# Two-layer decoder trunk with routed experts: the shared expert's first-tile up projection moved into the third quad of experts

## The reference, cut to what matters

```
def moe_ffn(x, router_w, router_b, w_gate, w_up, w_down, s_gate, s_up, s_down):
    scores = sigmoid(x @ router_w)                    # 64 experts, 8 groups
    ...                                               # 4 groups, then 8 experts for each token
    for each expert e and its tokens:
        hb = silu(xb @ w_gate[e]) * (xb @ w_up[e])    # 1024 -> 256
        y[tok] += (hb @ w_down[e]) * gate             # 256 -> 1024
    shared = (silu(x @ s_gate) * (x @ s_up)) @ s_down
    return y + shared
```

## Time and profile before

| what | value |
|---|---|
| median of three runs | 1256.37 us |
| profiled execution | 1257.92 us |
| its span in the profile | 1256.2 us |
| TensorE busy | 1201.1 us (96%) |
| VectorE, ScalarE busy | 397.9 us, 293.9 us |
| mean granted TensorE clock | 0.989 |
| read from HBM | 445.75 MB, 356 GB/s over the span |

### The profile page before, as it was taken

One profiled execution on the slowest core, in us unless ns is written; L12 is line 12 of the kernel. 1 busy time (PEld: TensorE's weight loads), 2 busy tenths in 40 slices (PEclk: granted clock), 3 DMA queues, 4 the chain that ended last, 5 costly groups with the idle time before them and its releaser, 6 DMA issues.

```text
span 1256.2 us, 17136 instructions
## 1 busy us (share of the span) xinstructions
PE 1201.1 (96%) x6956; PEld 560.9 (45%) x6956; DVE 397.9 (32%) x892; ACT 293.9 (23%) x648; POOL 28.5 (2%) x104
## 2 busy tenths in 40 slices
PE   8998999999999999999979999999999999999995
PEld 5776753434343434434336565343434333343431
DVE  3666374212221212222143656421212211221214
ACT  3354331112121212211122343111212111121212
POOL 1005000000000000000000000000000000000000
PEclk9999999999999999999989999999999999999998
DMA  9408068999999999999993657799999999999993
GB/s 369 167 12 330 6 246 368 416 426 425 430 427 426 428 427 427 428 428 428 428 380 106 268 201 293 292 409 429 430 426 428 429 424 429 427 426 430 428 426 131
DMA packets 45024, 447.72 MB, mean 356 GB/s; under 512 B 8096, under 2 KB 9504, under 8 KB 18848
## 3 DMA queue, kind: packets, MB, share of 16 engines
q1 hardware_dynamic: 44368, 446.29, 84.9%
q10 hardware_dynamic: 592, 0.53, 0.2%
HBM read 445.75 MB, written 1.05 MB: 356 GB/s over the span
## 4 chain that ended last, share of the span: by engine, by line
PE 83%; DMA 8%; DVE 5%; ACT 2%; issue 1%; DVEq 0%; SPq 0%
PE psum L411 32%; PE psum L516 16%; DMA w_up_ring<-in_moe_up 8%; PE psum L497 5%; PE psum L427 4%; PE psum L2376 4%; PE psum L2225 4%; PE psum L1246 3%; PE psum L614 2%; PE psum L476 2%; PE psum L648 1%; PE psum L1729 1%; PE psum L2382 1%; PE psum L1557 1%; DVE moe_h L1083 1%
## 5 line engine op out<-in xcount | busy, mean ns | idle before, releaser
L411 PE MATMUL psum<-w_up_ring,moe_x_selected 128*64 128x512 f32 x2048 | 452.8, 593 | 7.6 <-DMA w_up_ring<-in_moe_up 7.5
L411 PEld LDWEIGHTS psum<-w_up_ring,moe_x_selected 128*64 128x64 f32 x2048 | 149.3, 137 | 298.9 <-issue 286.3
L516 PE MATMUL psum<-w_down_ring,moe_hT 128*64 128x512 f32 x960 | 219.2, 598 | 0.0
L1083 DVE SCALAR_TENSOR_TENSOR moe_h<-moe_silu,moe_slot_gate,psum 128x256 f32<-128x256 f32 x64 | 30.7, 480 | 392.7 <-ACT moe_silu L834 392.5
L834 ACT ACTIVATE moe_silu<-psum 128x256 f32<-128x256 f32 x64 | 24.6, 384 | 429.7 <-PE psum L411 429.7
L516 PEld LDWEIGHTS psum<-w_down_ring,moe_hT 128*64 128x64 f32 x960 | 65.2, 136 | 123.4 <-issue 107.4
L1088 DVE TENSOR_TENSOR moe_out_low<-psum,moe_out_high 128x512 fp32r<-128x512 f32 x64 | 44.2, 691 | 213.1 <-ACT moe_out_high L846 213.1
L846 ACT CAST moe_out_high<-psum 128x512 fp32r<-128x512 f32 x64 | 37.5, 585 | 129.3 <-PE psum L516 129.3
L1090 DVE TENSOR_TENSOR moe_out_low<-psum,moe_out_high 128x512 fp32r<-128x512 f32 x64 | 44.2, 690 | 63.6 <-ACT moe_out_high L848 63.6
L427 PE MATMUL psum<-moe_match,moe_x_high 128*128 128x256 f32 x224 | 60.9, 307 | 2.8 <-ACT moe_x_selected L823 2.8
L497 PE MATMUL psum<-moe_out_high,moe_matchT 32*128 32x512 f32 x496 | 62.4, 494 | 0.0
(11 more groups left out here) (536 smaller groups left out, 1062.5 us busy)
## 6 DMA issues: line engine op xcount, KB each, us to landing
w_up_ring<-in_moe_up SPq DMA_DIRECT2D x128, 2048.0 KB, 16.5
w_down_ring<-in_moe_down SPq DMA_DIRECT2D x60, 2048.0 KB, 16.6
w_up_ring<-in_ev_columns SPq DMA_DIRECT2D x4, 2048.0 KB, 17.3
w_up_ring<-in_od_w_in SPq DMA_DIRECT2D x4, 2048.0 KB, 17.6
w_up_ring<-in_ev_out SPq DMA_DIRECT2D x2, 2048.0 KB, 8.1
moe_first_down<-in_moe_down SPq DMA_DIRECT2D x2, 2048.0 KB, 10.0
w_up_ring<-in_od_w_out SPq DMA_DIRECT2D x2, 2048.0 KB, 7.7
ln_gain_bias<-in_ln_g SPq DMA_DIRECT2D x4, 512.0 KB, 7.0
```

The costliest lines, as they stand in the source:

```text
L411: last = nc.tensor.matmul(k.psum[e * SLOTS:(e + 1) * SLOTS, 6, :], xsel[:, kk, own:own + SLOTS], up_view(par, e, kk), start=kk == 0, stop= ...
L516: last = nc.tensor.matmul(k.psum[e * SLOTS:(e + 1) * SLOTS, bank, :], hT[:, j * P + e * SLOTS:j * P + (e + 1) * SLOTS], places[e][:, j, ha ...
L1083: nc.vector.scalar_tensor_tensor(h[:], silu[:], slot_gate[:, i:i + 1], up_ps[:, FE:2 * FE], ALU.mult, ALU.mult).then_inc(s.h, 1)
```

## The change

Tile 0's up projection of the shared expert leaves the routing and `first_pair()`. It is done in one piece of eight matmuls in quad 2 (`SHARED_FIRST`), ahead of `pe_up` of pair i=1, in the way in which tile 1's is done in quad 3, and in the same bank 5. ACT's silu and DVE's product move there too. In layer 0 the transfer of the weights is issued after the fourth pair's second down weights. Quad 2 is written out; the loop ahead of it has one turn left. In `first_pair()` the transposition of the matching (L482) now stands ahead of the wait for `h`. In layer 1 no transfer moves; the matmuls move as in layer 0.

```diff
-SHARED_UP, SHARED_DOWN = 3, 4
+SHARED_FIRST, SHARED_UP, SHARED_DOWN = 2, 3, 4
...
-    shared_bank = (1, 5)
+    shared_bank = 5
...
         mixer.over(sp)
-        if layer == 0:
-            sp.dma_start(shared_w[:].rearrange("p a k f -> p (a k f)"), d.shared_up[layer]).then_inc(s.shared_w, 16)
         load_down_pair(sp, first_down[:], d, layer, 0, x.dn_first)
...
         load_down(sp, fourth_down[1], d, layer, 3, 1, x.dn_tokens)
+        if layer == 0:
+            sp.dma_start(shared_w[:].rearrange("p a k f -> p (a k f)"), d.shared_up[layer]).then_inc(s.shared_w, 16)
...
         logits(0)
-        pe.wait_ge(s.shared_w, 16)
-        shared_up(0, range(0, 2))
         turn_x(1)
         logits(1)
         places(0)
-        shared_up(0, range(2, 4))
...
-        shared_up(0, range(4, 5))
         pe.wait_ge(s.parts, NT)
...
             pe_slot_gates().then_inc(s.slot_gates, 1)
-            shared_up(0, range(5, KD)).then_inc(s.shared_up, 1)
+            pe_turn_match().then_inc(s.match_turned, 1)
             pe.wait_ge(s.h, 1)
             pe_turn().then_inc(s.turned, 1)
-            pe_turn_match().then_inc(s.match_turned, 1)
...
+            if peeled(q, SHARED_FIRST) and i == 1:
+                pe.wait_ge(s.matchT, q + 1)
+                pe.wait_ge(s.shared_w, 16)
+                shared_up(0).then_inc(s.shared_up, 1)
             if peeled(q, SHARED_UP) and i == 1:
                 pe.wait_ge(s.matchT, q + 1)
-                shared_up(1, range(KD)).then_inc(s.shared_up, 1)
+                shared_up(1).then_inc(s.shared_up, 1)
...
-            if first and i == 1:
-                pe.wait_ge(s.shared_h, 1)
...
+            if peeled(q, SHARED_FIRST) and i == 2:
+                pe.wait_ge(s.shared_h, 1)
...
-        with pe.Fori(1, SHARED_UP) as q:
+        with pe.Fori(1, SHARED_FIRST) as q:
...
-        for q in (SHARED_UP, SHARED_DOWN):
+        for q in (SHARED_FIRST, SHARED_UP, SHARED_DOWN):
...
+            if peeled(q, SHARED_FIRST) and i == 1:
+                shared_silu(0)
...
         take_silu(0)
-        shared_silu(0)
...
+            if peeled(q, SHARED_FIRST) and i == 1:
+                shared_h(0)
...
         gated_h(0, 0)
-        shared_h(0)
         overflow_table()
```

More of the change, by code:

```diff
@@ L610, in logits, with shared_up @@
             last.then_inc(s.logits, 1)
-        def shared_up(t, rows):
-            for kk in rows:
-                last = nc.tensor.matmul(k.psum[:, shared_bank[t], :], k.xT[:, kk, t * P:(t + 1) * P], shared_w[:, :, kk, :],
+        def shared_up(t):
+            for kk in range(KD):
+                last = nc.tensor.matmul(k.psum[:, shared_bank, :], k.xT[:, kk, t * P:(t + 1) * P], shared_w[:, :, kk, :],
                                         start=kk == 0, stop=kk == KD - 1)
@@ L817, in shared_silu @@
             act.wait_ge(s.shared_up, t + 1)
-            nc.scalar.activation(ssilu[:, t, :], k.psum[:, shared_bank[t], 0:FE], ACT.Silu).then_inc(s.shared_silu, 1)
+            nc.scalar.activation(ssilu[:, t, :], k.psum[:, shared_bank, 0:FE], ACT.Silu).then_inc(s.shared_silu, 1)
         def take_selected(taken):
@@ L876, in scalar @@
             pair(0, i)
-        with act.Fori(1, SHARED_UP) as q:
+        with act.Fori(1, SHARED_FIRST) as q:
             for i in range(4):
                 pair(q, i)
-        for q in (SHARED_UP, SHARED_DOWN):
+        for q in (SHARED_FIRST, SHARED_UP, SHARED_DOWN):
             for i in range(4):
@@ L980, in shared_h @@
             dve.wait_ge(s.shared_silu, t + 1)
-            nc.vector.tensor_tensor(sh[:, t, :], ssilu[:, t, :], k.psum[:, shared_bank[t], FE:2 * FE],
+            nc.vector.tensor_tensor(sh[:, t, :], ssilu[:, t, :], k.psum[:, shared_bank, FE:2 * FE],
                                     ALU.mult).then_inc(s.shared_h, 1)
@@ L1116, in vector @@
             pair(0, i)
-        with dve.Fori(1, SHARED_UP) as q:
+        with dve.Fori(1, SHARED_FIRST) as q:
             for i in range(4):
                 pair(q, i)
-        for q in (SHARED_UP, SHARED_DOWN):
+        for q in (SHARED_FIRST, SHARED_UP, SHARED_DOWN):
             for i in range(4):
```

## The result

| | before | after |
|---|---|---|
| median of four runs each | 1256.57 us | 1265.64 us |
| lowest and highest | 1255.67, 1257.50 | 1264.71, 1266.02 |
| profiled execution, its span | 1257.92, 1256.2 us | 1265.40, 1263.5 us |
| mean granted clock | 0.989 | 0.982 |

The ratio is 1.0071, with a 95% interval from 1.0058 to 1.0084. The forecast was 1257.9 us, "no difference", with a range up to 1261.8 us. Both the time and the sign of the answer were wrong.

The account below looks back on a forecast made before the run. DMA transfers and PE were taken as nearly level limits in the expert phases. Layer ends 1.4 and 0.1 us later gave +1.5 us, 1259.4 us on the profiled execution, 1257.9 us against the median; range 1253.8 to 1261.8 us.

Parts of the forecast that it names:

- Routing, worth nothing: Five matmuls removed from the routing gain zero, since PE would have stood idle there until DVE was ready.
- rival (1): PE's clock falls in the routing without the shared matmuls, costing 1.6 us a layer: 1261.0 us; chance 0.24.
- First pair, 1.7 us gained in each layer: Three matmuls removed from the first pair let the down matmuls start 1.7 us earlier, shrinking the hole in the transfers.
- Moved transfer, nothing: Issuing layer 0's 2 MB transfer at its batch's end changes nothing, bounds 2.3 us either way.
- Quad 2, PE 7.1 us later: Eight matmuls added in quad 2 make PE 7.1 us later, 5.4 us after the first pair's gain, in each layer.
- Do the DMA engines run dry: After quad 2, the scarcest transfer lands 0.8 us later in layer 0, 0.4 us earlier in layer 1.
- How much does the end take up: PE's waiting at layer ends absorbs 4.05 and 5.35 us of its 5.4 us lateness, leaving 1.4 and 0.1 us.
- The sum: Both layers together end 1.5 us later; against the median 1257.9 us, "no difference"; chance 0.55.
- (2) to (4): Rivals: transfers decide all the way, 1253.0 us, 0.12; first pair gains nothing, 1261.3 us, 0.06; end absorbs nothing, 1267.2 us, 0.03.
- What would show it: Signs: time to landing falls about 7 us from quad 2, to 7 or 8 at quad 5; end waits nearly vanish.

Follow-up runs that it names:

- e1: The changed kernel with five filler matmuls, whose results nobody reads, where the shared matmuls had stood in the routing; 1261.48 us.
- e4: The kernel before without the three shared matmuls in the first pair, the matching's transposes moved ahead of the wait for `h`, nothing added in quad 2; 1253.23 us.
- e12: The changed kernel with layer 0's transfer of the shared up weights issued first again, as before; 1264.89 us.
- e9: The changed kernel with the five routing fillers, and the shared expert's three parts in quads 3, 5 and 6 in place of 2, 3 and 4; 1257.59 us.
- e5: The kernel before with eight more matmuls, result not read, ahead of `pe_up` of pair i=1 in quad 6; 1261.19 us.
- e6: The kernel before with four more matmuls, result not read, ahead of `pe_up` of pair i=1 in quad 6; 1258.06 us.
- e3: The kernel before with eight more matmuls, result not read, in quad 2 where the change puts its block; 1264.94 us.
- e2: The changed kernel with the five routing fillers and only the first of the eight matmuls in quad 2, in both layers; 1255.53 us.
- e8: The kernel before with the first pair's three shared matmuls moved, one into the routing and two into first-pair waits, quad 2 left in its loop; 1253.47 us.

## Why the prediction was wrong

**Routing, worth nothing: wrong in what it took for cover.** PE did wait for DVE in all three places, as the step said (1.48 us at 180.66). What the matmuls did there besides, hold the clock, the step priced at nothing and left to rival (1), at 0.24. The fall came as that rival put it. Its size was taken from the mean clock of another stretch, 1.6 us a layer; the runs showed 3.24 and 0.95, together 4.2 (and 4.2 by the medians, change less e1), against the rival's 3.1. "The clock held with gaps half as long" was no evidence against it: those gaps stood beside dense work. The Trainium skill, "TensorE: Matmul & The Clock Gate", section "What's actually happening", has the slow clock as the default and activity as what lifts it; e1 agrees, at 1.00 with the fillers and 0.50 without them.

**First pair, 1.7 us gained in each layer: right.** 1.71 and 1.72 us in the change, kept to the end in e4: 3.1 us by the medians.

**Moved transfer, nothing: right,** by e12's trace, within some 0.2 us at the refill behind it.

**Quad 2, PE 7.1 us later: right.** 7.0 us, the pairs 19.62 us apart, 7.04 us for the `pe_up` behind it.

**Do the DMA engines run dry: the step that failed for the rest, 3.9 us by the medians of e1 and e9.** It put the transfer at 481.9 us at 0.8 us later than before and looked for one hole, at the scarcest transfer. In the change that transfer is issued at 489.9 and lands at 489.9 + 8.8 = 498.7: 5.0 us later than 493.7. The step's rule, issue + 7.2, would give 497.1: 3.4 us later, 2.6 of them since PE was 8.0 us late there and not 5.4. The other 1.6 us are the loss that the rule hasn't. And the transfers before it had lost time already. The one at 388.5 lands 1.8 us later than its fellow of before (380.5, landing after 13.7), the one at 397.6 2.7, the one at 432.9 4.7 us (before: 424.9, 13.3). The last shows the fault best. The transfer ahead of it, issued at 427.4, lands after 8.9 us, at 436.3. The rule has the next land at the later of 432.9 + 7.2 = 440.1 and 436.3 + 4.9 = 441.2. It landed at 442.9, 1.7 us beyond the later. Time to landing of those issued at 427.4 and 424.9 us, in the change and before:

```profile
DMA to landing us min/median/max: 8.9/8.9/8.9
...
DMA to landing us min/median/max: 13.3/13.3/13.3
```

With 13.3 us to landing, before, its fellow had landed 4.9 us behind its own predecessor. The others are alike: the one at 397.6, issued 3.3 us before the landing ahead of it, landed 5.8 us behind that; the one at 489.9, issued 2.5 us before, 6.3 us behind. Each lost 0.9 to 1.7 us although one transfer was still in flight; the one at 388.5, the thinnest, lost 0.3. The step had looked for one loss and taken the largest; there were several, and they add up. By the landings of quads 3 to 5 they come to 3.6 us in layer 0 (from +2.0 to +5.6) and 4.0 in layer 1 (from -2.1 to +1.9).

**How much does the end take up: right as a rule, wrong here.** PE's lateness less 4.05 and 5.35 us of waiting holds in e5 (2.95 and 1.67) and in e9, and within about 1 us in e6. In the change PE's lateness was 8.5 and 6.2 us, the clock's part included. But the stream of transfers had become late on its own, so PE still waited 1.13 and 1.05 us at the last half, and the ends were 5.62 and 1.90 us late, where the rule with the right lateness gives 4.45 and 0.85. The text had called a wait at the end a sign that it was wrong; the waits it looked at did go, from 7.5 to 2.2 us, and the last was enough.

**The sum.** Forecast +1.5 us; with the clock's 4.2 (change less e1) and the place's 3.9 (e1 less e9) it is +9.6, measured +9.1. Each of the two sizes is sure to some 2 us only, so that the sum comes so near is partly luck. e9 without both came out at +1.4. In the profiled executions alone the place shows as 2.5 us, (2.45 + 0.98) - (1.13 - 0.21); single executions differ by as much as what is missing, and I don't assign it to a place. The forecast also took 1.55 us off, since the profiled execution of before lay that far above its median. The change's own profiled execution lies 0.24 us below its median, so such an excess isn't handed on.

**Rivals.** The mechanism of (1) came, and (2) to (4) didn't. Its time, 1261.0 us, is what the clock would give together with the rest of the forecast; the case that came, (1) and a second step mis-sized, was in none of them. The chances had them as alternatives. The upper bound of 1261.8 should have held (1) on top of a block at e3's cost.

**What would show it.** The time to landing did fall by 6 to 7 us right behind the block (388.5: 7.5 in place of 13.7; 327.0: 9.9 in place of 16.4), but at the start of quad 5 only by 3, from 11.8 to 8.8. That is the same thing as the loss: PE was 8 us later there, and the transfers had become 5 us later with it.

**Open.** e2 and e4 both take the block away and keep the first pair's gain, yet differ by 2.3 us (1255.53 and 1253.23). e2 has one matmul more in quad 2, a peeled loop and the moved transfer; these weren't taken apart. By their landings from the second half of quad 2 on, e2 lost 5.5 us in both layers together and e4 2.9, none of it behind a thin queue; why isn't known. Why some transfers that are issued with one other in flight land late, and others hardly, wasn't measured by itself either.

## What to carry to other kernels

Before taking matmuls out of a wait, ask what else PE has in that stretch: here five matmuls that cost nothing kept the clock up through a routing of 16 us that is otherwise small work. Where an engine and the transfers run level, work moved into the middle has two prices, its own lateness and what the transfers lose once their time to landing comes near that of an empty queue; read the GB/s row, not the DMA row in tenths, and put the work where the queue is neither thin nor full, or better into waits that exist (e8). Causes found in one profile can both be true: add them before setting the upper bound.

## What the runs showed of the hardware that was not expected

The granted clock, once at 0.50, stayed there for 13.7 us in layer 0 of the change and 6.9 us in layer 1 though PE was busy for 11.48 of 13 us (transposes and matmuls of 64 and 256 columns), and came back only with `pe_up` in layer 0; in e12, the same routing, it stayed some 10 us both times.

2 MB transfers lost throughput before the queue was empty: 413 GB/s over 100 us in place of 427, with 7.5 to 13.6 us to landing in the change, where a transfer issued 3.4 us before its predecessor landed came 6.6 us behind it in place of 4.9. Not every such transfer lost time, and single ones lost as much behind a full queue (before, at 1036.9 us: 6.6 us behind its predecessor, with 17.8 us to landing).
